# Norm factors sent across partitions by two transfers through memory in three places, with two first gate products ordered by width

## The reference

```python
# first block
h = rmsnorm(x, norm_mix_pre);  x = x + rmsnorm(mixer(h, ...), norm_mix_post)
h = rmsnorm(x, norm_ffn_pre);  x = x + rmsnorm(swiglu(h, w_gate_up, w_down), norm_ffn_post)
# second block
x = x + 0.5 * swiglu_2(rms_norm(x, norm_ffn1), ffn1_w1, ffn1_w3, ffn1_w2)
x = x + hybrid_mixer(rms_norm(x, norm_mix), w_in, ...)
x = x + memory_attention(rms_norm(x, norm_mem_q), rms_norm(mem, norm_mem_kv), ...)
x = x + 0.5 * swiglu_2(rms_norm(x, norm_ffn2), ffn2_w1, ffn2_w3, ffn2_w2)
x = rms_norm(x, norm_out)

def rms_norm(x, g):
    return x * rsqrt(mean(x * x, axis=-1, keepdims=True) + 1e-6) * g
def swiglu_2(h, w1, w3, w2):
    return (silu(h @ w1) * (h @ w3)) @ w2          # hidden width 2816
```

## Time and profile before

| | before |
|---|---|
| median of 3 runs | 964.27 us |
| lowest and highest run | 964.21, 964.28 us |
| the profiled execution, its own time | 964.19 us |
| its span, first to last instruction | 962.4 us |
| granted clock of TensorE, of full speed | 0.998 |
| PE busy | 99% of the span |
| DVE busy | 693.4 us, 72% |
| ACT busy | 504.5 us, 52% |
| transfers | 178.82 MB, 186 GB/s in the mean |

### The profile page before, as it was taken

The page is one execution under the profiler, slowest core; times in us unless marked ns, Lnnn a source line. Parts: engine busy times, 40 slices in busy tenths (PEclk is TensorE's granted clock), DMA queues, the critical chain, the costliest instruction groups (busy, mean ns, idle before and its releaser), DMA issues.

```text
span 962.4 us, 13313 instructions
## 1 busy us (share of the span) xinstructions
PE 955.5 (99%) x5174; PEld 825.8 (86%) x5174; DVE 693.4 (72%) x725; ACT 504.5 (52%) x689; POOL 20.0 (2%) x21
## 2 busy tenths in 40 slices
PE   9999999999999999999999999999999999999997
PEld 9888888888888888888888888899888888888886
DVE  5779758857776768886767776685676587767676
ACT  5454676663434344834343346574978554343434
POOL 1001000031000000000000000000000000000000
PEclk9999999999999999999999999999999999999999
DMA  7955486655565667655555563745445445656551
GB/s 242 289 169 175 158 258 220 232 182 175 176 216 174 218 175 219 202 162 198 193 195 186 182 211 132 230 142 175 150 157 197 131 132 177 216 174 218 174 175 44
DMA packets 139811, 178.82 MB, mean 186 GB/s; under 512 B 25770, under 2 KB 108156, under 8 KB 139644
## 3 DMA queue, kind: packets, MB, share of 16 engines
q1 hardware_dynamic: 139052, 175.86, 56.0%
q10 hardware_dynamic: 720, 2.43, 0.6%
HBM read 175.65 MB, written 1.05 MB: 184 GB/s over the span
## 4 chain that ended last, share of the span: by engine, by line
PE 99%; DVE 1%; ACT 0%; issue 0%; DVEq 0%; ACTq 0%
PE gate_banks L756 13%; PE up_banks L756 12%; PE bank L512 9%; PE bank L513 9%; PE bank L514 9%; PE up_banks L512 7%; PE up_banks L513 7%; PE up_banks L514 7%; PE up_banks L761 7%; PE gate_banks L761 7%; PE up_banks L618 3%; PE up_banks L623 2%; PE bank L678 1%; PE gate_banks L831 1%; PE bank L696 1%; PE bank L902 0%
## 5 line engine op out<-in xcount | busy, mean ns | idle before, releaser
L1755 DVE TENSOR_TENSOR w_lo<-stage,w_hi 128x2048 fp32r<-128x2048 f32 x81 | 185.4, 2289 | 96.5 <-ACT w_hi L1194 96.5
L1749 DVE TENSOR_TENSOR w_lo<-stage,w_hi 128x2048 fp32r<-128x2048 f32 x78 | 178.3, 2288 | 64.2 <-ACT w_hi L1187 64.0
L1187 ACT ACTIVATE w_hi<-stage 128x2048 fp32r<-128x2048 f32 x79 | 151.0, 1912 | 66.1 <-PE up_banks L623 20.6
L1194 ACT ACTIVATE w_hi<-stage 128x2048 fp32r<-128x2048 f32 x81 | 152.5, 1905 | 0.0
L756 PE MATMUL gate_banks<-act_both,w_hi 128*128 128x512 f32 x528 | 129.6, 391 | 0.0
L756 PE MATMUL up_banks<-act_both,w_hi 128*128 128x512 f32 x528 | 125.6, 390 | 0.0
L756 PEld LDWEIGHTS up_banks<-act_both,w_hi 128*128 128x128 f32 x528 | 98.7, 188 | 20.1
L756 PEld LDWEIGHTS gate_banks<-act_both,w_hi 128*128 128x128 f32 x528 | 95.7, 188 | 17.3
L1269 ACT ACTIVATE ffn_hi<-gate 128x512 fp32r<-128x512 f32 x30 | 19.0, 633 | 156.8 <-DVE gate L1885 156.8
L512 PE MATMUL bank<-w_hi,ffn_hi 128*128 128x512 f32 x240 | 93.8, 391 | 0.0
L513 PE MATMUL bank<-w_lo,ffn_hi 128*128 128x512 f32 x240 | 93.7, 391 | 0.0
(11 more groups left out here) (405 smaller groups left out, 1487.4 us busy)
## 6 DMA issues: line engine op xcount, KB each, us to landing
stage<-in_ffn_w SPq DMA_DIRECT2D x66, 1024.0 KB, 5.3
stage<-in_w_in SPq DMA_DIRECT2D x33, 1024.0 KB, 5.3
stage<-in_w_gate_up SPq DMA_DIRECT2D x22, 1024.0 KB, 5.1
stage<-in_w_down SPq DMA_DIRECT2D x11, 1024.0 KB, 4.9
stage<-in_w_out SPq DMA_DIRECT2D x8, 1024.0 KB, 6.1
stage<-in_mem_w_kv SPq DMA_DIRECT2D x8, 1024.0 KB, 5.3
stage<-in_w_branch SPq DMA_DIRECT2D x4, 1024.0 KB, 5.5
stage<-in_mem_w_q SPq DMA_DIRECT2D x4, 1024.0 KB, 5.6
```

Of the source, the lines that this page charges most:

```text
L1187: act.activation(w_hi[:, place, :], stage[:, place, :], copy).then_inc(hi_done, 1)
L1194: act.activation(w_hi[:, place, :], stage[:, place, :], copy).then_inc(hi_done, 1)
L1749: dve.tensor_tensor(w_lo[:, place, :], stage[:, place, :], w_hi[:, place, :].bitcast(F32), ALU.subtract).then_inc(lo_done, 1)
L1755: dve.tensor_tensor(w_lo[:, place, :], stage[:, place, :], w_hi[:, place, :].bitcast(F32), ALU.subtract).then_inc(lo_done, 1)
```

## The change

In the first feed-forward, the second feed-forward and the second mixer, spread, factor_rows and rows_out are removed. SP does their work with two transfers: it writes the 256 factors from norms to a small tensor in device memory (sent), waits until they have landed, and reads them back as one row repeated over the 128 partitions into rs. The place is in SP's own order: after the first down chunk of each feed-forward (its first turn is taken out of the loop for that) and after the value chunks DV of the second mixer. DVE's waits on rs_done there become waits on rs_landed. The first gate products of the first and second feed-forward wait for all eight blocks of act_lo and then run by width. The first mixer and the last feed-forward keep the way of before.

```diff
-ROWS = [N_X0, N_FFN0, N_FFN1, N_MIX2, N_FFN2]
+ROWS = [N_X0, N_FFN2]
+SENT = [N_FFN0, N_FFN1, N_MIX2]
...
+        sent = nc.dram_tensor("sent", (len(SENT), T), F32, kind="Internal").ap()
...
+            def send_row(i):
+                sp.wait_ge(r_done, SENT[i] + 1)
+                sp.dma_start(sent[i].rearrange("(t p) -> p t", p=P), factors[SENT[i]], allow_slow_non_contiguous=True).then_inc(row_sent, 16)
+                sp.wait_ge(row_sent, 16 * (i + 1))
+                if i:
+                    sp.wait_ge(silu_scaled, PAIRS * i)
+                else:
+                    wait_scaled(sp, HC + 1)
+                sp.dma_start(rs[:, :], sent[i:i + 1, :].to_broadcast([P, T])).then_inc(rs_landed, 16)
...
-                with sp.Fori(0, PAIRS - 2) as t:
+                def turn(t, after_down=None):
                     c = base + 2 + t * 3
                     whole(c, w_g, t * 256 + (g_col + 256), slot(base + 2))
                     rows(c + 1, w_d, t * 256, 2, 0, D, slot(base + 3))
+                    if after_down is not None:
+                        after_down()
                     whole(c + 2, w_u, t * 256 + (u_col + 256), slot(base + 4))
+
+                turn(0, sent_row)
+                with sp.Fori(1, PAIRS - 2) as t:
+                    turn(t)
...
                 if c in TOKEN_PAIRS:
                     token_pair(c, w_in2, col)
+                    if c == DV:
+                        send_row(2)
...
                 aux(A_BEFORE_FFN[f])
-                halves_product(gate_banks, base % RING, act_lo_done, 8 * prep, between)
+                if f == 2:
+                    halves_product(gate_banks, base % RING, act_lo_done, 8 * prep, between)
+                else:
+                    pe.wait_ge(act_lo_done, 8 * prep + 8)
+                    halves_product(gate_banks, base % RING)
+
                 def rows():
                     factor_rows(ROWS.index(norm), ACC)
-                if f < 2:
-                    rows()
...
-                    if first:
+                    if first and f == 2:
                         pe.wait_ge(rs_done, ROWS.index(norm) + 1)
...
             up_tok(DQ, act_hi, act_lo, 0, act_lo_done, 32)
-            factor_rows(ROWS.index(N_MIX2), SUM)
             up_tok(DQ, act_hi, act_lo, 1, act_lo_done, 32)
...
-            rows_out(N_FFN0, ACC)
...
-            rows_out(N_FFN1, ACC)
...
-            rows_out(N_MIX2, SUM)
...
+                    elif f < 2:
+                        dve.wait_ge(rs_landed, 16 * (f + 1))
                     else:
-                        dve.wait_ge(rs_done, (1, 2, 4)[f] + 1)
+                        dve.wait_ge(rs_done, 2)
...
-            spread(N_FFN0)
...
-            spread(N_FFN1)
...
-            spread(N_MIX2)
...
-            dve.wait_ge(rs_done, 4)
+            dve.wait_ge(rs_landed, 48)
             scaled(RQ, rq_T[:, 0:2, :], rs)
```

More of the change, by code:

```diff
@@ L285, in build @@
         rows_landed, stored = sem("rows_landed"), sem("stored")
+        row_sent, rs_landed = sem("row_sent"), sem("rs_landed")
         nat_done = [sem(f"nat_done{i}") for i in range(2)]
+        sent = nc.dram_tensor("sent", (len(SENT), T), F32, kind="Internal").ap()
         block = ctx.enter_context(nc.Block())
@@ L387, in token_pair, with feed_forward @@
                     rows(c + i, w, 512 * i, 4, col, 512, slot(c + i))
-            def feed_forward(base, w_g, g_col, w_u, u_col, w_d, between=None):
+            def feed_forward(base, w_g, g_col, w_u, u_col, w_d, between=None, sent_row=None):
                 whole(base, w_g, g_col, slot(base))
                 whole(base + 1, w_u, u_col, slot(base + 1))
-                with sp.Fori(0, PAIRS - 2) as t:
+                def turn(t, after_down=None):
                     c = base + 2 + t * 3
@@ L464, in key_blocks @@
                                      ).then_inc(keys_landed, 16)
-            feed_forward(FFN[0], a["w_gate_up"][0], 0, a["w_gate_up"][0], HID, a["w_down"][0], key_blocks)
+            feed_forward(FFN[0], a["w_gate_up"][0], 0, a["w_gate_up"][0], HID, a["w_down"][0], key_blocks, lambda: send_row(0))
             token_pair(MEMV[0], a["mem_w_kv_2"][0], D)
-            feed_forward(FFN[1], a["ffn1_w1_2"][0], 0, a["ffn1_w3_2"][0], 0, a["ffn1_w2_2"][0])
+            feed_forward(FFN[1], a["ffn1_w1_2"][0], 0, a["ffn1_w3_2"][0], 0, a["ffn1_w2_2"][0], sent_row=lambda: send_row(1))
             token_pair(MEMV[1], a["mem_w_kv_2"][0], D + 512)
```

## The result

| | before | after |
|---|---|---|
| median | 964.24 us (4 runs) | 977.77 us (4 runs) |
| lowest and highest run | 964.11, 964.28 us | 977.67, 977.96 us |
| span of the profiled execution | 962.4 us | 975.8 us |

The changed kernel is slower: the ratio of the times is 1.014, with a 95% interval of 1.0128 to 1.0152. That is 13.5 us more, where 1.4 less were forecast.

A forecast was written before the change was run, and what follows sets the result against it. The prediction took PE's own instruction stream as the bound: 964.19 - 1.37 = 962.82 us for the profiled execution, and 0.08 more for the median gave 962.9 us. The range was 962.3 to 964.4.

The forecast's parts named there:

- PE's stream is the time; 1.37 us leave it.: Three places: removed factor-row matmuls and the order by width shorten PE's stream by 0.46, 0.45 and 0.46 us.
- The order by width costs nothing and gives 0.03 us a place.: First gate products of both feed-forwards: 5.54 us by width against 5.57 alternating; waiting for all eight blocks costs nothing.
- DVE's and ACT's removed steps cost and give nothing.: All three places: the removed diagonals and PSUM copy leave engines that wait for PE, so the time stays.
- I take 1.9 for a write on idle queues, 2.5 for a read.: SP's queue, all three places: prices in us, from 48 earlier transfers of 256 pieces (32 KB), best 1.9, median 2.5.
- the point of decision: Second feed-forward: write and read together may take 10.1 us before the gate scaling comes too late for PE.
- latest scaling of 216.0: First feed-forward: latest time of DVE's gate scaling that still gives PE its low part in time; slack 5.1 us.
- The far row of 9.8 us: Time of 1024 pieces of 32 bytes in the crowded start, used as each transfer's price in the slower rival.
- A write behind a chunk lands 1.9 us after it.: SP's queue: a write following a 1 MB weight chunk lands 1.9 us after that chunk, whose landing takes 5.1.
- In the mixer SP is 2.5 us late, with a slack of at least 3.6; nothing reaches PE.: Second mixer: SP reaches the query blocks at 610.7, not 608.16; transposes and low part end before PE's scores at 629.63.
- the small write is dear: Slower rival: 4-byte pieces make the first feed-forward 5.4 us late, the second 9.5, mixer mostly hidden; 977.8 us, chance 0.07.
- an estimate of 4.3 for the pair: By the skill's fixed time per transfer, write and read together take some 4.3 us; PE's sum stays the same.

The follow-up runs named there:

- the kernel without transfers: The changed kernel with both transfers and DVE's wait removed, rs keeping the first mixer's factors in the three places; 963.01 us, ratio 0.9987.
- with 8 bytes: The changed kernel with each partition's two factors written side by side, 128 pieces of 8 bytes instead of 256 of 4; 966.47 us.
- the run on chip: The changed kernel with the write sent to one SBUF partition as two transfers of 128 4-byte pieces, and the read taking an input row; 963.90 us.

## Why the prediction was wrong

The predicted 962.9 us, with a range of 962.3 to 964.4, was 14.9 us under the measurement, and no change was forecast where the kernel became 1.4% slower.

1. *PE's stream is the time; 1.37 us leave it.* Right: 11.11 us in both feed-forwards, 1.27 us by the medians of the kernel without transfers.
2. *The order by width costs nothing and gives 0.03 us a place.* Right, by the kernel with the order alone.
3. *DVE's and ACT's removed steps cost and give nothing.* Nothing speaks against it: the kernel without transfers shows only the saving.
4. *"I take 1.9 for a write on idle queues, 2.5 for a read."* **This step failed**, and it is the larger failure. The write took 7.7 us, the read 6.2, 13.9 together in the second feed-forward, where the text itself put the point of decision at 10.1. 13.9 - 10.1 = 3.8 us late, and the gap is 3.88. In the first the pair took 9.1 + 6.1 from 201.67 on and rs was there at 216.87, against a latest scaling of 216.0: 0.9 late, gap 1.00. The slacks of the feed-forwards were right to a tenth; only the prices were not. The rows they came from the earlier trace rows are pieces of 128 bytes, and they say nothing of pieces of 4 bytes side by side. The far row of 9.8 us was kept as a price but given 0.07.
5. *A write behind a chunk lands 1.9 us after it.* Failed by the same price alone: 9.1 us behind one chunk and 10.7 behind two, where 7.0 was forecast; with 8 bytes it is 6.7 and 7.1.
6. *In the mixer SP is 2.5 us late, with a slack of at least 3.6; nothing reaches PE.* **This step failed too, and not by the price alone.** The query blocks began at 620.69 instead of 608.16. Of these 12.5 us, 5.7 are the shift that the feed-forwards had left, and 6.8 are the mixer's own. The transposes, at 634.98, let PE stand 1.45 us, and the retention chunks behind them were late in turn. But the slack was wrong as well. The text let SP be 2.5 + 3.6 = 6.1 us late before PE would stand. With 8 bytes the last query block is issued just 6.1 us later than before (36.40 against 30.28 in the table), and PE has stood 2.96 us by then. The text followed the transposes and the low part right behind them. It left out the second chunk of retention queries, which SP issues only behind the 16 blocks, and DVE's work behind that chunk; and it kept 10.41 us for the 16 issues, which took 11.4 to 13.4 behind a read of one row. Even on its own start (22.4 in the table, that of the run on chip, 22.43) PE stood 0.64 us.
7. *The half clock was not in the sum.* No row of before showed PE standing 2 us or more, so none could price it. It cost 1.74 us in the second feed-forward, and about 1.7 of the 2.61 left over in the mixer (an estimate, from 5 us at 0.66).

The rival "the small write is dear" had the mechanism and its two points of decision. Its time, 977.8, agrees with 977.77 only by chance: it had 5.4, 9.5 and nothing for the three places, less the saving; measured were 0.65, 5.17 and 7.69 net, which is 1.11, 5.62 and 8.15 before the saving. It had the pair at 19.6 us, two fifths too much, called the mixer hidden and left the clock out, and these errors cancel. Its chance of 0.07 rested on rows of larger pieces, which are no evidence for pieces of 4 bytes.

The Trainium skill ("DMA: Bandwidth & Descriptors", Anatomy of one DMA) by its 2.0 us fixed, which it gives for transfers issued by GpSimd, led to an estimate of 4.3 for the pair. The spaced write (1.5) and the one on chip (2.0) agree with that size; the packed one (7.7) doesn't, and the measurement decides.

What stays open: why the row of sent is read in 5.6 to 6.2 us and the row of an input mostly in 3.9 to 4.7; what makes the granted clock fall after one stand and not after another of the same length; and about 0.3 us of the 2.61 in the mixer.

## What to carry to other kernels

When an operation that no row shows enters a chain with a few us of slack, the range has to reach to where it decides: here 10.1 us for two transfers stood in the text beside one row of 9.8 us, and the chance given to that side was far too small. By these runs, values spread over partitions go to device memory better in pieces of 8 bytes or spaced apart than as 4-byte pieces side by side, and the queue that issues the weights should not wait for their landing: issue the write, go on with the chunks, read later. When a queue is held, follow every transfer behind the hold to its reader, not only the next one: here the chunk behind the 16 small transfers set the loss. Where a stand of PE is forecast, a case with half clock behind it belongs in the range: here it added 1.7 us to a stand of 3.7.

## What was not expected of the hardware

- Write of the factors to device memory, on idle queues: 7.7 us for 256 pieces of 4 bytes side by side, 7.7 for 128 such, 2.7 to 2.8 for 128 pieces of 8 bytes, 1.5 for 256 pieces of 4 bytes 64 bytes apart.
- Read of 128 KB to 128 partitions, all places of all runs on SP's queue: 2.2 and 2.3 us from 128 different rows, and once 5.2; 3.9 to 4.7 from one row of an input, and twice 5.4 to 5.6; 5.6 to 6.2 from the row written before.
- The packed write from POOL: 11.0 us, against 7.7 from SP.
- The granted clock at 0.50 for 3 us after a stand of 3.7 us, again for some 3 us after stands of 0.97 and 2.20, and not after one of 0.85, nor in the 8-byte kernel after 0.76 and 2.20.
- The same 16 small issues on SP's queue took 10.4 us before, 11.0 without the transfers, and 13.0 to 13.4 behind a read of one row of sent. Behind a read of different rows they took 10.7.
- A multiply on DVE whose factors are read with a step of two elements took no longer: 0.69 us for 128x512, as with adjacent ones.
